# Stick-breaking sweep: scores as three 64-row products, transposes in two row halves, one eviction for each head's piece

## The reference

```
z = einsum('bhtd,bhsd->bhts', qh[:, :, t0:t1], kh[:, :, :t1]) * scale
mask = arange(t1)[None, :] < (t0 + arange(QBLOCK))[:, None]
log_keep = where(mask, log_sigmoid(-z), 0.0)
rc = lax.cumsum(log_keep, axis=3, reverse=True)      # suffix sums over the keys
after = concatenate([rc[..., 1:], zeros_like(rc[..., :1])], axis=-1)
w = where(mask, exp(log_sigmoid(z) + after), 0.0)
out = einsum('bhts,bhsd->bhtd', w, vh[:, :, :t1])
```

## Time and profile before

| | us |
|---|---|
| median of 3 runs | 3042.92 (3042.72 to 3047.29) |
| the profiled execution | 3037.94 |
| its span | 3036.2 |
| the sweep: first product of L1340 to last row of L1410 | 1787.5 to 2617.7 |

### The profile page before, as it was taken

The page is one execution under the profiler, slowest core; times in us unless marked ns, Lnnn a source line. Parts: engine busy times, 40 slices in busy tenths (PEclk is TensorE's granted clock), DMA queues, the critical chain, the costliest instruction groups (busy, mean ns, idle before and its releaser), DMA issues. The chain is left out here.

```text
span 3036.2 us, 53001 instructions
## 1 busy us (share of the span) xinstructions
PE 2805.4 (92%) x20640; PEld 2377.8 (78%) x20640; DVE 1872.7 (62%) x1922; ACT 1258.3 (41%) x2057; POOL 624.0 (21%) x397
## 2 busy tenths in 40 slices
PE   8899999998899999997676769999999999799998
PEld 6688888886787888886666668888888888678887
DVE  4755544436655543443788868878978897654343
ACT  5233323333233333332122147777767777521111
POOL 1422222223422222220755410000000000000000
PEclk9999999999999999998999989999999999899999
DMA  7345543334345533334454552452345231342221
GB/s 303 122 138 166 167 125 104 94 108 153 98 138 152 169 120 105 109 91 148 141 168 150 159 143 74 119 141 57 98 127 136 61 85 43 115 150 104 83 83 42
DMA packets 260109, 370.69 MB, mean 122 GB/s; under 512 B 12449, under 2 KB 193057, under 8 KB 242977
## 3 DMA queue, kind: packets, MB, share of 16 engines
q1 hardware_dynamic: 259392, 366.87, 39.2%
q10 hardware_dynamic: 480, 0.53, 0.1%
HBM read 245.72 MB, written 121.64 MB: 121 GB/s over the span
## 5 line engine op out<-in xcount | busy, mean ns | idle before, releaser
L569 PE MATMUL b_ps<-hc_hi,w 128*128 128x512 f32 x3584 | 930.0, 395 | 34.4 <-issue 15.2
L569 PEld LDWEIGHTS b_ps<-hc_hi,w 128*128 128x128 f32 x3584 | 666.9, 189 | 174.7 <-issue 23.8
L569 PE MATMUL b_ps<-hc_lo,w 128*128 128x512 f32 x1792 | 485.3, 393 | 0.0
L1466 DVE TENSOR_TENSOR_SCAN run<-akeep,later_row 128x768 f32<-128x768 f32 (+7 forms) x256 | 410.9, 1649 | 98.7 <-ACT akeep L1433 94.7
L689 DVE TENSOR_TENSOR u<-b_ps,u 128x512 f32<-128x512 f32 x320 | 220.3, 688 | 385.3 <-PE b_ps L569 384.8
L569 PEld LDWEIGHTS b_ps<-hc_lo,w 128*128 128x128 f32 x1792 | 339.3, 189 | 73.4
L1422 ACT ACTIVATE wt<-t_ps 128x512 f32<-128x512 f32 (+3 forms) x640 | 314.2, 536 | 146.6 <-PE t_ps L1352 146.5
L1352 PE MATMUL t_ps<-ident,run 128*128 128x128 f32 x2176 | 312.4, 278 | 6.8 <-DVE run L1466 6.1
L1433 ACT ACTIVATE akeep<-z_ps 128x1024 f32<-128x1024 f32 (+7 forms) x384 | 280.5, 778 | 36.1 <-PE z_ps L1341 32.9
L1372 PE MATMUL o_ps<-wt,ad 128*64 128x128 f32 x4352 | 280.0, 277 | 9.0 <-issue 9.0
L1352 PEld LDWEIGHTS t_ps<-ident,run 128*128 128x128 f32 x2176 | 244.4, 141 | 51.0 <-issue 28.1
(11 more groups left out here) (157 smaller groups left out, 3512.7 us busy)
## 6 DMA issues: line engine op xcount, KB each, us to landing
w_raw<-in_w_in SPq DMA_DIRECT2D x64, 1024.0 KB, 6.0
aq<-s_qhi SPq DMA_DIRECT2D x64, 256.0 KB, 5.9
aq<-s_qlo SPq DMA_DIRECT2D x64, 256.0 KB, 6.2
o<-s_o SPq DMA_DIRECT2D x16, 1024.0 KB, 5.9
h_raw<-in_w_ada SPq DMA_DIRECT2D x8, 1024.0 KB, 7.4
xg<-in_x SPq DMA_DIRECT2D x4, 2048.0 KB, 14.8
s_gq<-u SPq DMA_DIRECT2D x32, 256.0 KB, 5.0
s_gf<-u SPq DMA_DIRECT2D x32, 256.0 KB, 3.7
```

The costliest lines, as they stand in the source:

```text
L569: mm = nc.tensor.matmul(bank[:, :], wt[:, n % 2, j, k * P:(k + 1) * P], ht[:, j, k * 512:(k + 1) * 512], start=(j < 4 and c == 0), stop=(c ...
L1466: nc.vector.tensor_tensor_scan(dst, stay[:, ::-1], later[:, D - width:D][:, ::-1], 1.0, ALU.mult, ALU.max).then_inc(run_ready, 1)
```

## The change

It does four things.

1. The tile q now holds the 64 rows of head 0 in partitions 0 to 63 and of head 1 in 64 to 127, once for the high and once for the low part, and so does k. A score is now three products over 64 rows (hi·hi, hi·lo, lo·hi), and the two heads take turns: head 0 in the upper row half of TensorE, head 1 in the lower, each into its own `z_ps`.
2. A transpose of a 128 x 128 block is now two, one for queries 0 to 63 and one for 64 to 127, each from its row half, with a 64 x 64 piece of the identity as the moving operand. They write two banks of one `t_ps` of 1024 columns.
3. There is one eviction for each head's piece, up to 1024 wide. With one `t_ps`, the transposes of a head's piece wait until the eviction before it is done (`wt_ready`), on an added semaphore instruction (`turning`). The order of the steps is as before.
4. The loads follow: 2 DMAs of 512 KB for a half of q, 2 of 1 MB for k; in `hgrn` the two ahead of q now come before those of k.

```diff
+    HQ = P // 2
-        wt = m.sb("wt", [P, 8, 512])
+        wt = m.sb("wt", [P, 4, 2, 512])
-        t_ps = [m.ps(f"t_ps{a}", [P, 512]) for a in range(2)]
+        t_ps = m.ps("t_ps", [P, D])
...
-                def scores(i, n, e):
+                def scores(i, n):
...
-                        nc.tensor.matmul(zz, q_hi, kk, start=True, stop=False)
-                        mm = nc.tensor.matmul(zz, q_lo, kk, start=False, stop=True)
-                    mm.then_inc(z_ready, 1)
+                        for j, (qp, kp) in enumerate(((0, 0), (0, 1), (1, 0))):
+                            for e in range(2):
+                                rows = slice(e * SD, (e + 1) * SD)
+                                if a == 0 and j == 0:
+                                    pe.wait_ge(keep_ready, i * (2 * PP) + (2 * n + e + 1))
+                                mm = nc.tensor.matmul(z_ps[e][:, a:a + wd], q[rows, qb // 8, qp, toks], k[rows, b, kp, lo + a:lo + a + wd],
+                                                      start=(j == 0), stop=(j == 2))
+                                if a + wd == width and j == 2:
+                                    mm.then_inc(z_ready, 1)
...
                     pe.wait_ge(run_ready, i * (2 * PP) + (2 * n + e + 1))
-                    src = run[:, e, qb % 2, home(qb):]
-                    for a, key, wd in part_list(n, e):
-                        if a >= 2:
-                            pe.wait_ge(wt_ready, i * (4 * NS) + (a - 1))
-                        for j in range(wd // P):
-                            mm = nc.tensor.transpose(t_ps[a % 2][:, j * P:(j + 1) * P], src[:, key + j * P:key + (j + 1) * P],
-                                                     keep["ident"][:, :])
-                        mm.then_inc(t_ready, 1)
+                    if 2 * n + e >= 1:
+                        pe.wait_ge(wt_ready, i * (2 * PP) + (2 * n + e))
+                    nc.tensor.sem_inc(turning, 1)
+                    src = run[:, e, qb % 2, home(qb) + lo:home(qb) + lo + width]
+                    for j in range(width // P):
+                        for h in range(2):
+                            rows = slice(h * HQ, (h + 1) * HQ)
+                            mm = nc.tensor.transpose(t_ps[:, h * 512 + j * HQ:h * 512 + (j + 1) * HQ], src[rows, j * P:(j + 1) * P],
+                                                     keep["ident"][rows, rows])
+                    mm.then_inc(t_ready, 1)
...
                     def evict(e):
-                        for a, key, wd in part_list(n1, e):
-
-                            act.wait_ge(t_ready, i * (4 * NS) + (a + 1))
-                            nc.scalar.activation(wt[:, a % 8, 0:wd], t_ps[a % 2][:, 0:wd], ACT.Identity, scale=-1.0,
-                                                 bias=1.0).then_inc(wt_ready, 1)
+                        half = at(n1)[3] // 2
+                        act.wait_ge(t_ready, i * (2 * PP) + (2 * n1 + e + 1))
+                        nc.scalar.activation(wt[:, (2 * n1 + e) % 4, :, 0:half], t_ps[:, :].rearrange("p (h n) -> p h n", h=2)[:, :, 0:half],
+                                             ACT.Identity, scale=-1.0, bias=1.0).then_inc(wt_ready, 1)
...
                 def load_q(i, b, h):
                     toks = slice(h * D, (h + 1) * D)
-                    for e in range(2):
-                        for part in range(2):
-                            for dup in range(2):
-                                dst = q[dup * SD:(dup + 1) * SD, h, e, part, :].bitcast(F32)
-                                sp.dma_start(dst, scr["sq"][part][rows_of(i, b, e), toks]).then_inc(q_in[h], 16)
+                    for part in range(2):
+                        sp.dma_start(q[:, h, part, :].bitcast(F32), scr["sq"][part][cols_of(i, b), toks]).then_inc(q_in[h], 16)
```

More of the change, by code:

```diff
@@ L923, in _ @@
                 sp.dma_start(keep["later"][:, :], io["later"]).then_inc(ahead["later_in"], 16)
-                for e in range(2):
-                    sp.wait_ge(q_level, count(n_two - 1, 1, 2 * NLEV, 4))
-                    sp.wait_ge(k_level, count(n_two - 1, 1, KL, 2))
-                    for part in range(2):
[L929 to L935, removed]
-                        for dup in range(2):
-                            sp.dma_start(ahead["q"][dup * SD:(dup + 1) * SD, 0, e, part, :].bitcast(F32),
-                                         scr["sq"][part][e * SD:(e + 1) * SD, 0:D]).then_inc(ahead["q_in"][0], 16)
+                sp.wait_ge(mm_ready[0], count(n_two - 1, 0, MB, MB))
+                sp.wait_ge(mm_ready[1], count(n_two - 1, 0, MB, MB))
+                for part in range(2):
+                    sp.dma_start(ahead["q"][:, 0, part, :].bitcast(F32), scr["sq"][part][0:P, 0:D]).then_inc(ahead["q_in"][0], 16)
+                sp.wait_ge(q_level, count(n_two - 1, 1, 2 * NLEV, 4))
+                sp.wait_ge(k_level, count(n_two - 1, 1, KL, 2))
+                for part in range(2):
+                    sp.dma_start(ahead["k"][:, 0, part, :].bitcast(F32), scr["sk"][part][0:P, :]).then_inc(ahead["k_in"][0], 16)
                 for e in range(2):
@@ L1159, in stick @@
     PP = 2 * NP
-    parts = [[(lo + a, min(512, width - a)) for a in range(0, width, 512)] for _, lo, width in pieces]
-    before = [sum(len(x) for x in parts[:n]) for n in range(NP)]
-    NS = sum(len(x) for x in parts)
+    HQ = P // 2
     group_end = [max(n for n in range(NP) if pieces[n][0] // 4 == g) for g in range(4)]
@@ L1195, in stick @@
         t_ready = m.sem("t_ready")
+        turning = m.sem("turning")
         wt_ready = m.sem("wt_ready")
@@ L1209, in at @@
             return (n // NP % 2,) + pieces[n % NP]
[L1211 to L1218, removed]
         def home(qb):
@@ L1251, in load_q @@
                     toks = slice(h * D, (h + 1) * D)
-                    for e in range(2):
-                        for part in range(2):
-                            for dup in range(2):
-                                dst = q[dup * SD:(dup + 1) * SD, h, e, part, :].bitcast(F32)
-                                sp.dma_start(dst, scr["sq"][part][rows_of(i, b, e), toks]).then_inc(q_in[h], 16)
+                    for part in range(2):
+                        sp.dma_start(q[:, h, part, :].bitcast(F32), scr["sq"][part][cols_of(i, b), toks]).then_inc(q_in[h], 16)
                 def load_k(i, b):
[L1259 to L1262, removed]
+                    for part in range(2):
+                        sp.dma_start(k[:, b, part, :].bitcast(F32), scr["sk"][part][cols_of(i, b), :]).then_inc(k_in[b], 16)
                 def load_v(i, b):
@@ L1324, in _ @@
                 nc.tensor.sem_inc(r_ready, 1)
-                def scores(i, n, e):
+                def scores(i, n):
                     b, qb, lo, width = at(n)
[L1328 to L1333, removed]
+                    if n % NP == 0:
+                        pe.wait_ge(k_in[b], i * 32 + 32 * (n // PP + 1))
+                        pe.wait_ge(q_in[0], i * 64 + 32 * (n // NP + 1))
+                    if n % NP == half_end + 1:
+                        pe.wait_ge(q_in[1], i * 64 + 32 * (n // NP + 1))
+                    toks = slice(qb % 8 * P, (qb % 8 + 1) * P)
@@ L1344, in transposes @@
                 def transposes(i, n, e):
[L1345 removed]
+                    qb, lo, width = at(n)[1:]
                     pe.wait_ge(run_ready, i * (2 * PP) + (2 * n + e + 1))
[L1347 to L1354 removed]
+                    if 2 * n + e >= 1:
+                        pe.wait_ge(wt_ready, i * (2 * PP) + (2 * n + e))
@@ L1358, in weighted @@
                     diag = lo + width == (qb + 1) * P
-                    lists = [part_list(n, e) for e in range(2)]
                     if diag and qb % 4 == 0:
@@ L1365, in weighted @@
                     cols = slice((qb % 4) * P, (qb % 4 + 1) * P)
[L1366 to L1374, removed]
+                    pe.wait_ge(wt_ready, i * (2 * PP) + (2 * n + 2))
+                    for j in range(width // P):
+                        for e in range(2):
+                            mm = nc.tensor.matmul(o_ps[e * SD:(e + 1) * SD, cols], delta[:, b, lo // P + j, e * SD:(e + 1) * SD],
+                                                  wt[:, (2 * n + e) % 4, :, j * HQ:(j + 1) * HQ], start=(diag and j == 0),
+                                                  stop=(lo == 0 and (j + 1) * P == width))
                     mm.then_inc(av_ready, 1)
@@ L1388, in step @@
                     if there(n, last):
-                        scores(i, n, 0)
-                        scores(i, n, 1)
+                        scores(i, n)
                     if there(n - LAG_T, last):
@@ L1459, in step @@
                                 free = max(x for x in range(n) if at(x)[1] == last_user)
-                                dve.wait_ge(t_ready, i * (4 * NS) + (last_part(free, e) + 1))
+                                dve.wait_ge(t_ready, i * (2 * PP) + (2 * free + e + 1))
                             if not diag:
```

(2 more changed lines are left out.)

6 lines of the change are left out of this document (removed).

## The result

The changed kernel takes 3029.99 us (median of 8 runs, 3021.54 to 3032.57), the kernel before 3042.39 (8 runs): ratio 0.996, 95% interval 0.9946 to 0.9973. That is 12 us faster where 27 or 28 were forecast. The profiled execution took 3032.57 us, its span is 3030.8.

The account below looks back on a forecast made before the run. TensorE was taken to bound the kernel at 100.9 us a pair; a loop through ACT would give 97.5. 3037.9 less 27 for eight pairs and 1 for loads is 3010, 3015 as median; whole range 2988 to 3104.

Parts of the forecast that it names:

- the loop: In each step, scores, two sigmoids, eviction and head 0's next transposes follow one another: 90.9 us a pair.
- The clock is no rival of its own: TensorE's granted clock would hold, since hgrn keeps 0.98 at 39 of 50 us busy; no time was allowed.
- TensorE bounds the kernel before: In the sweep, TensorE's work sums to 100.2 of 100.9 us a pair, the bound in nearly every step.
- Scores and transposes overlap in row halves: On TensorE, row halves run side by side: scores 23.9 us a pair, transposes 0.058 us a block.
- TensorE's sum: TensorE's own work for a pair after the change: 78.4 us, 22 us below today's, not expected to come out.
- 97.5 us a pair: Forecast time of a pair of heads in the changed sweep, 3.4 us below 100.9.
- The 3 us for late scans: Allowance per pair for DVE scans sometimes waited for with pieces of unlike width; bounds 0 and 6 us.
- 3.6 us for these: Per pair, narrow steps: 2.2 us for TensorE's longer side, 1.4 us for head 0 evictions holding sigmoids up.
- Loads: Fewer q bytes and DMA issues save 1 us at the start, between 0 and 3; in hgrn zero.
- A change of tiling costs 0.15 us: Two changes a step on TensorE between transposes and column halves: 48 x 0.15 = 7.2 us a pair.
- 24 us either way: Width of the forecast's own range, given as 2998 to 3038, from late scans costing 0 to 6 us a pair.

Follow-up runs that it names:

- e9: The kernel before, with only the eviction of head 1 on ScalarE moved between the two sigmoids: 3041.34 us, ratio 1.0003.
- e2: The kernel before, with GpSimd's difference of v left out for six of eight pairs of heads: 3036.82 us, ratio 0.9995.
- e3: The changed kernel, with the eviction of head 1 on ScalarE moved between the two sigmoids: 2980.78 us, ratio 0.9804.
- e4: The changed kernel, with the transposes of head 0 done twice in every step: 3083.55 us, ratio 1.0149.
- e1: The changed kernel, with GpSimd's difference of v left out for six of eight pairs of heads: 3017.35 us, ratio 0.9934.
- e7: The changed kernel, with the transposes of head 1 done twice in twelve steps where TensorE waits anyway: 3020.83 us, ratio 0.994.
- e10: The changed kernel in its own order, with the difference of v moved from GpSimd to DVE, in four pieces after the first pair: 3013.22 us, ratio 0.9921.
- e5: The kernel before with only the change's scores and loads; transposes whole, two banks, one eviction a part, as before: 3062.73 us, ratio 1.0077.
- e6: The kernel before with only the change's row-half transposes, one t_ps and one eviction; scores and loads as before: 3039.09 us, ratio 0.9993.

## Why the prediction was right and wrong

The direction held, and the loop is there; the size did not hold. The step of the prediction that failed is "The clock is no rival of its own", and with it the hiding of single long waits behind TensorE's queue.

- *TensorE bounds the kernel before:* right. e9 and e2 leave it where it is.
- *Scores and transposes overlap in row halves:* right. 0.23 a pair of scores as taken, 0.060 to 0.065 a block for transposes against 0.058.
- *A loop over both sigmoids, the eviction and the next transposes:* right, and shown by e3 against e9 and by e4. It does not bind in every step: of the 191 sets of transposes of head 0 behind the first, 107 wait for the eviction and 5 for a scan, and in 79 TensorE comes to them without having stood still. The rule of the Trainium skill (TensorEngine Tiling (Array Packing), "PSUM Bottleneck") had the direction: of 22 us a pair that TensorE's sum lost, 2.3 came out.
- *97.5 us a pair:* measured 98.6, 9 us in the sweep. Of the 1.1 us, 0.7 is the transposes' price (136 x 0.005). That the sum came so near is partly luck. The 3 us for late scans were not needed for scans: in e1 only one of 382 sets of transposes waits for one, and its pair is still 98.5. They went into steps where pieces of unlike width meet, in most of which TensorE comes to the transposes without having stood still; the prediction had counted 3.6 us for these, and which part of the queues is late there no run shows.
- *"no row prices that. I take 3 us":* the trace of before did have one, outside the rows read. A scan beside GpSimd takes 4 us too long there as well. I had priced DVE by its busy share, in which such a hold-up hides, and had taken its cover, TensorE's own queue, for granted after taking 22 us out of that queue.
- *"The clock is no rival of its own":* the step that failed. I argued from the mean of 50 us in hgrn (39 busy at 0.98). The mean in the changed sweep is higher, 85 of 100, and the clock fell ten times, behind standstills of 0.8 to 3.3 us; the mean does not tell. Together, falls and held-up scans cost 17 us more than the accidents of the kernel before in the profiled execution (about two thirds of it the clock, by the estimate at e7), and 8 to 12 by the ratios of e1 and e10 against that of the changed kernel. The forecast had nothing for the clock.
- *Loads:* the sweep starts 0.9 us earlier in its first product (1786.6 to 1787.5), and the first weighted sum comes at 1801.0 against 1802.8. As taken.
- *A change of tiling costs 0.15 us:* the number of changes stays in the whole change, so the price drops out; in e5 and e6 the two added ones cost 0.26 and 0.21 us together.
- *Slips in the sums:* the two sigmoids are 28.5 us a pair by the stated price, not 28.7, and 24 us either way around 3015 reaches down to 2991, not 2998. Neither changes the argument.

27 forecast for the sweep, less 9 for the steps and 17 for the accidents, is the 1 us by which the profiled sweeps differ (829.0 against 830.2). The timings, 12 us, are kinder than that one execution, by fewer falls of the clock and by up to 4 us outside the sweep that no run here takes apart.

## What to carry to other kernels

When TensorE's work is cut, follow every wait that its queue used to hide, one by one and at its longest, not by the mean: here a scan held up for 4 us by GpSimd had been free and was no longer. The order of the engine that empties PSUM has to be chosen anew with such a change; one moved eviction gave 47 us, four times what the change itself gave, and nothing in the kernel before. And look at the kinds of product that alternate: here moving only one of two into row halves cost 5 to 6 us a pair in changes of tiling, and moving both cost none of them.

## What the runs showed of the hardware

- A DVE scan and a GpSimd subtraction that run at the same time hold each other up: two scans take 7.68 us beside 4.57 us of GpSimd, and 3.41 without it; in the kernel before GpSimd's own took 5.05 beside them.
- TensorE's granted clock fell to 0.50 behind a stretch with 1.10 of 3.00 us busy, although the mean was 85%. Taking the GpSimd work away left two of ten falls in the profiled execution, and so did adding products off the path that nobody needs.
- Two fp32 transposes of 64 rows in the two row halves run side by side, loads of 128 columns included, at 0.060 to 0.065 us, and products of 64 rows by 512 columns at 0.23 a pair.
- Between products of 128 and of 64 rows TensorE lost 0.21 to 0.26 us for two changes (e5, e6), and nothing where both kinds had 64 rows.
